# Four rounded weight buffers, the low part written over the raw tile, bias rows in three pieces

## What is computed

```python
def first_block(...):
    for i in range(DEPTH):
        j = i // N_MIXERS
        if i % N_MIXERS == 0:
            mix = retention(x, ret_w_in[j], ret_w_out[j])
        else:
            mix = dilated_attention(x, attn_w_in[j], attn_w_out[j], rel_bias)
        x = _layer_norm(DEEPNORM_ALPHA * x + mix, ln_gain[i, 0], ln_bias[i, 0])
        x = _layer_norm(DEEPNORM_ALPHA * x + swiglu_ffn(x, ffn_w_up[i], ffn_w_down[i]),
                        ln_gain[i, 1], ln_bias[i, 1])
    return x

def second_block(...):
    for l in range(DEPTH):
        h = rms_norm(x, norm1_g[l])
        proj = h @ w_in[l]
        ...
        mixed = jnp.concatenate([y_att, y_conv.astype(x.dtype), y_rnn.astype(x.dtype)], axis=-1)
        x = x + mixed @ w_out[l]
        h2 = rms_norm(x, norm2_g[l])
        x = x + peer(h2, peer_wq[l], peer_k1[l], peer_k2[l], peer_u[l], peer_v[l])
    return rms_norm(x, final_g)
```

## Time and profile before

| | |
|---|---|
| median of 3 runs | 2896.3 us (2894.7 to 2897.42) |
| profiled execution | 2887.31 us, span of the profile 2885.5 us |
| granted TensorE clock, mean | 0.994 |
| TensorE, VectorE, ScalarE busy | 2796.1, 1916.6, 1558.9 us |
| DMA | 480.26 MB, 166 GB/s over the span |

### The profile page before, as it was taken

One profiled execution on the slowest core, in us unless ns is written; L12 is line 12 of the kernel. 1 busy time (PEld: TensorE's weight loads), 2 busy tenths in 40 slices (PEclk: granted clock), 3 DMA queues, 4 the chain that ended last, 5 costly groups with the idle time before them and its releaser, 6 DMA issues.

```text
span 2885.5 us, 51650 instructions
## 1 busy us (share of the span) xinstructions
PE 2796.1 (97%) x18787; PEld 2539.2 (88%) x18787; DVE 1916.6 (66%) x3175; ACT 1558.9 (54%) x2817; POOL 22.7 (1%) x37
## 2 busy tenths in 40 slices
PE   8999999999999989999999999998999999999998
PEld 7988988898998879999998888887999999988886
DVE  5655554555555868987886555578699678855555
ACT  4455454555545564447775444456544677644444
POOL 0000000000000000000000000000000000000000
PEclk9999999999999999999999999999999999999999
DMA  6445557664555444554444555543455444455554
GB/s 231 147 146 180 187 167 194 173 165 143 168 184 165 131 136 164 179 175 139 140 139 163 192 191 189 190 164 110 160 172 179 156 143 141 140 196 190 191 192 146
DMA packets 158723, 480.26 MB, mean 166 GB/s; under 512 B 14608, under 2 KB 51472, under 8 KB 158192
## 3 DMA queue, kind: packets, MB, share of 16 engines
q1 hardware_dynamic: 154080, 460.38, 48.3%
q0 software_dynamic: 4352, 17.53, 2.8%
q10 hardware_dynamic: 144, 0.34, 0.0%
HBM read 477.02 MB, written 1.18 MB: 166 GB/s over the span
## 4 chain that ended last, share of the span: by engine, by line
PE 89%; DVE 6%; ACT 3%; issue 1%; DMA 0%; ACTq 0%; POOL 0%; DVEq 0%; POOLq 0%
PE ps L1570 27%; PE ps L1572 27%; PE ps L1571 26%; PE ps L2087 4%; DVE wl L872 2%; ACT wh L404 2%; DVE arena L1261 1%; PE ps L1689 1%; DVE xr L891 1%; PE ps L2053 0%; PE ps L1827 0%; PE ps L1870 0%; ACT arena L465 0%; DVE arena L1142 0%; DMA xr<-x_dram 0%
## 5 line engine op out<-in xcount | busy, mean ns | idle before, releaser
L872 DVE TENSOR_TENSOR wl<-raw,wh 128x1024 fp32r<-128x1024 f32 x878 | 1075.5, 1225 | 865.4 <-ACT wh L404 858.4
L404 ACT ACTIVATE wh<-raw 128x1024 fp32r<-128x1024 f32 x878 | 930.0, 1059 | 1235.0 <-PE ps L1572 1229.3
L1570 PE MATMUL ps<-xh,wh 128*128 128x256 f32 x3920 | 1135.5, 290 | 6.5 <-DVE wl L872 4.3
L1571 PE MATMUL ps<-xl,wh 128*128 128x256 f32 x3920 | 1110.2, 283 | 0.0
L1572 PE MATMUL ps<-xh,wl 128*128 128x256 f32 x3920 | 1109.6, 283 | 0.0
L1570 PEld LDWEIGHTS ps<-xh,wh 128*128 128x128 f32 x3920 | 752.2, 192 | 23.0 <-issue 10.7
L1571 PEld LDWEIGHTS ps<-xl,wh 128*128 128x128 f32 x3920 | 753.3, 192 | 0.3
L1572 PEld LDWEIGHTS ps<-xh,wl 128*128 128x128 f32 x3920 | 752.2, 192 | 0.0
L1570 PE MATMUL ps<-wh,mh 128*128 128x512 f32 x1304 | 513.5, 394 | 3.7 <-DVE ml L884 2.0
L1572 PE MATMUL ps<-wh,ml 128*128 128x512 f32 x1304 | 510.1, 391 | 0.0
L1571 PE MATMUL ps<-wl,mh 128*128 128x512 f32 x1304 | 509.0, 390 | 0.0
(11 more groups left out here) (287 smaller groups left out, 2023.0 us busy)
## 6 DMA issues: line engine op xcount, KB each, us to landing
raw<-stream_dram SPq DMA_DIRECT2D x878, 512.0 KB, 3.3
arena<-bias_scratch POOLq DMA_DIRECT2D x16, 384.0 KB, 7.9
arena<-norm_rows POOLq DMA_DIRECT2D x4, 1024.0 KB, 7.7
arena<-keys_dram POOLq DMA_DIRECT2D x2, 1024.0 KB, 5.0
arena<-ret_c_dram POOLq DMA_DIRECT2D x1, 1344.0 KB, 7.9
xr<-x_dram POOLq DMA_DIRECT2D x1, 1024.0 KB, 8.1
out_dram<-arena POOLq DMA_DIRECT2D x2, 512.0 KB, 2.9
arena<-rg_w_dram POOLq DMA_DIRECT2D x2, 256.0 KB, 2.9
```

The costliest lines, as they stand in the source:

```text
L404: A(wh[b % 2][:, :, :], raw[:, b % 4, :].rearrange("p (a b) -> p a b", a=DB), ACT.Copy) \
L872: V.tensor_tensor(wl[b % 2][:, :, :], raw[:, b % 4, :].rearrange("p (a b) -> p a b", a=DB), wh[b % 2][:, :, :].bitcast(F32), ALU.subtract) ...
L1570: M(out_ap, lh, rh, start=first, stop=False, skip_group_check=skip)
L1571: M(out_ap, lh, rl, start=False, stop=False, skip_group_check=skip)
```

## The change

The three things that it does: `wh` and `wl` get four buffers each. The four of `wl` lie in the same memory as the four slots of `raw`, so the subtraction writes over the raw tile that it reads. A slot is therefore free for the next load only when the matmuls of its tile are done, and SyncE waits for `mm_done` in place of `w_lo`; `hi(b)` waits for `mm_done` of tile b-4. The bias of a head comes in three transfers of 128 KB, one for each group, each behind the split of a tile of its own (`w_lo`), on GpSimd's queue as before. The order of all other instructions stays.

```diff
-        raw = sb("raw", [4, TILE])
-        wh = [sb(f"wh{i}", [DB, P], F32R) for i in range(2)]
-        wl = [sb(f"wl{i}", [DB, P], F32R) for i in range(2)]
+        with nc.sbuf_tensor("raw", [P, 4, TILE], F32) as raw:
+            pass
+        low = sb("wl", [4, DB, P], F32R)
+        wl = [low[:, i, :, :] for i in range(4)]
+        wh = [sb(f"wh{i}", [DB, P], F32R) for i in range(4)]
...
                 for b, g in enumerate(sources, first):
-                    sp.wait_ge(w_lo, b - 3)
+                    sp.wait_ge(mm_done, b - 3)
                     load(b % 4, g)
...
                     for s in range(4):
-                        sp.wait_ge(w_lo, i * 4 + (s - 3))
+                        sp.wait_ge(mm_done, i * 4 + (s - 3))
                         load(s, i * 4 + s)
...
             for h in range(AH):
-                if h >= 4:
-                    pool.wait_ge(a_b, h - 3)
-                else:
-                    pool.wait_ge(w_lo, START["att"] + 12 + 4 * h)
-                pool.dma_start(bs[:, h % 4, :, :], bass.AP(
-                    scratch.tensor, h * 384, [[1, P], [AH * 384, G3], [1, T]])).then_inc(b_in[h % 4], 16)
+                for g in range(G3):
+                    if h >= 4:
+                        pool.wait_ge(a_b, h - 3)
+                        pool.wait_ge(w_lo, START["att"] + 29 + 6 * ((h - 2) // 2) + 3 * (h % 2) + g)
+                    else:
+                        pool.wait_ge(w_lo, START["att"] + 12 + 4 * (3 * h + g) // 3)
+                    pool.dma_start(bs[:, h % 4, g, :], bass.AP(
+                        scratch.tensor, (g * AH + h) * 384, [[1, P], [1, T]])).then_inc(b_in[h % 4], 16)
...
-                if b >= 2:
-                    act.wait_ge(mm_done, (b - 1) + n * body)
-                A(wh[b % 2][:, :, :], raw[:, b % 4, :].rearrange("p (a b) -> p a b", a=DB), ACT.Copy) \
+                if b >= 4:
+                    act.wait_ge(mm_done, (b - 3) + n * body)
+                A(wh[b % 4][:, :, :], raw[:, b % 4, :].rearrange("p (a b) -> p a b", a=DB), ACT.Copy) \
                     .then_inc(w_hi, 1)
...
-                V.tensor_tensor(wl[b % 2][:, :, :], raw[:, b % 4, :].rearrange("p (a b) -> p a b", a=DB),
-                                wh[b % 2][:, :, :].bitcast(F32), ALU.subtract).then_inc(w_lo, 1)
+                V.tensor_tensor(wl[b % 4][:, :, :], raw[:, b % 4, :].rearrange("p (a b) -> p a b", a=DB),
+                                wh[b % 4][:, :, :].bitcast(F32), ALU.subtract).then_inc(w_lo, 1)
...
-                dve.wait_ge(b_in[h % 4], 16 * (h // 4 + 1))
+                dve.wait_ge(b_in[h % 4], 16 * G3 * (h // 4 + 1))
```

More of the change, by code:

```diff
@@ L1587, in tile_a @@
                         pe.wait_ge(n_lo, split_before[norm] + c + 1)
-                    ins = passes(ps_t[:, e % 2, 0:T], (wh[b % 2][:, c, :], wl[b % 2][:, c, :]),
+                    ins = passes(ps_t[:, e % 2, 0:T], (wh[b % 4][:, c, :], wl[b % 4][:, c, :]),
                                  (xh[:, c, :], xl[:, c, :]), c == 0, c == DB - 1)
@@ L1600, in tile_b @@
                         ins = passes(ps_a[:, 2 * c + h, :], (mh[:, s, t], ml[:, s, t]),
-                                     (wh[b % 2][:, 4 * h:4 * h + 4, :].rearrange("p a b -> p (a b)"),
-                                      wl[b % 2][:, 4 * h:4 * h + 4, :].rearrange("p a b -> p (a b)")),
+                                     (wh[b % 4][:, 4 * h:4 * h + 4, :].rearrange("p a b -> p (a b)"),
+                                      wl[b % 4][:, 4 * h:4 * h + 4, :].rearrange("p a b -> p (a b)")),
                                      first, last, skip=True)
@@ L1611, in last_pair @@
                     t = slice(c * P, (c + 1) * P)
-                    s, w = 2 * (u % 2) + j, (b + j) % 2
+                    s, w = 2 * (u % 2) + j, (b + j) % 4
                     if (j, c, h) == (1, 0, 0):
@@ L1631, in out_part @@
                         ins = passes(ps_a[:, 2 * c + h, :], (high[:, t], low[:, t]),
-                                     (wh[b % 2][:, kb:DB:2, :], wl[b % 2][:, kb:DB:2, :]),
+                                     (wh[b % 4][:, kb:DB:2, :], wl[b % 4][:, kb:DB:2, :]),
                                      first and kb == 0, False, skip=True)
@@ L1641, in last_parts @@
                     high, low = mixed(2 * part + kb)
-                    t, w = slice(c * P, (c + 1) * P), (b + h) % 2
+                    t, w = slice(c * P, (c + 1) * P), (b + h) % 4
                     if (h, c, kb) == (1, 0, 0):
```

## The result

The changed kernel takes 2840.84 us in the median of four runs (2836.79 to 2845.78); the kernel before, beside it, 2895.77 (2894.70 to 2897.42). The ratio is 0.9812, 95% interval 0.9801 to 0.9824: 54.9 us faster. A second measurement gave 2839.43 against 2894.83, ratio 0.981 (0.9797 to 0.9824).

What follows compares the result with a forecast made beforehand. Matmuls were taken as the bound, TensorE being busy for 97% of the span. Terms of 39.4 us won and 4 lost, 35.4 net, took the profile from 2887.3 to 2852; 9.0 more gave a median of 2861, range 2847 to 2881.

Steps and rivals of the forecast that it cites:

- A: First attention: scaling starts some 2 us sooner, so transposes and scores stop waiting; 8.9 us won, ends 0 and 10.
- B: Mixed stage of each second-block layer: shorter waits of transposes, at start and end; 12.6 us won, ends 4 and 17.
- C: Picking experts: one tile of lead evens out VectorE's uneven lots; 7.6 us won over two layers, ends 0 and 9.
- D: First gates: one-hots start 2.6 us earlier, the matmuls' stall and some lowered clock go; 5.8 us won, ends 0 and 7.
- E: Tile starts: TensorE's waits for `wl` outside the mixed stages and the third tile; 1.5 us won, ends 0 and 2.
- F: Value tables and down projections: some late first weight loads go if `wl` is the reason; 3 us won, ends 0 and 7.
- G: Loads beside GpSimd's 1 MB transfers (gains at start and feed-forwards): less slack; 3 us lost, three places at 1 each.
- H: Bias pieces: a load beside one takes 5.0 us, under 5.8 allowed; 1 us lost, ends 0 and 4.
- Only the tiles themselves gain: Rival: softmax chains get work sooner, but something else in the in-order queues comes last; 2880 us, chance 0.18.
- Buffers change nothing: Rival: `evacuate`, not the semaphore, holds `hi` everywhere, so only noise remains; 2896 us, chance 0.06.
- Loads become the bound: Rival: load, rounding and subtraction close a loop over three tiles; 2993 us at landings of 6.7 us, chance 0.06.
- the turning point: Landing time of loads, 6.4 us held over all 878 tiles, at which slower loads would cancel the 39 us won.

## Why the prediction was wrong

By its own terms, with the same stages of the two profiled executions, and of the second pair (the kernel before again, the changed one again, on two chips). Won is positive:

| term | predicted | first pair | second pair |
|---|---|---|---|
| A, first attention | 8.9 | 9.7 | 9.8 |
| B, mixed stages | 12.6 | 11.9 | 16.2 |
| C, picking | 7.6 | 9.9 | 9.8 |
| D, first gates | 5.8 | 5.9 | 7.8 |
| E and F, tile starts, tables, projections | 4.5 | 13.4 | 15.9 |
| G and H, feed-forwards, keys, bias | -4 | -1.9 | -1.3 |
| norms, first load, landing of the output | 0 | -1.1 | -1.3 |
| sum of the spans | 35.4 | 47.8 | 56.9 |

**The mechanism was right.** The lead of the rounding is the whole gain (2898.44 us without it), one tile of it is enough (2840.77 with three buffers), and each named sign is there: transposes, scores and gates no longer wait, the mixed stage keeps one long wait a layer, the feed-forward tile stays at 2.88 us (852 matmuls in 120 us, 851 before), some roundings wait for a landing, and a tile near the start of each feed-forward waits. The subtraction takes as long in place (1224 ns). One sign of being wrong came too, once: beside the bias pieces a load took 6.1 us where 5.8 were allowed, in the attention's values, and TensorE waited 0.35 us there.

**The step that failed is term F.** The prediction put it as "the first weight load of a tile comes late in 58 places, 10.0 us, most of it under matmuls that still run", took 3 and closed the term at 7. The two tables of values alone gave 8.2 us (10.5 in the second pair), retention 3.6 (4.0), and the first tiles of the tables 1.6: with E 13.4, 8.9 more than predicted, by far the largest miss. Its question, the late `wl` or the loop, is answered: the late `wl` (with and without the lead 1457 and 1439 matmuls in 330 us). What it missed is where the cost lies. In the first table before the change there are 227.9 ns in the mean between the matmuls on both sides of a tile's boundary, hardly more than the usual 226.5. The next interval is 259 once in every four tiles, and many of those behind it are 229 to 236. Worked out from the trace, the table takes 4.9 us more than 226.5 ns a matmul: 0.2 at the boundaries, 0.7 at one wait inside the last pair of tiles, 4.1 spread inside the tiles. Before, the low part was ready 0.23 us ahead of its tile in the median, now 2.1. The waits view shows the late weight loads but not this cost, for TensorE doesn't idle. The reading that would have: the smallest interval found anywhere between two such matmuls, times their count, against the stage's time. It should also have been applied to retention (16 + 16 tiles) and to the change from stage to stage, which the term left out. The feed-forward's tiles had 0.36 us of lead before, and between start and end of the stage six tiles take 16.98 us in place of 17.00: there the tile did gain nothing, as predicted.

**The second step is the one from the profile to the median.** It read "the median of the runs shown, 2896.3, lies 9.0 above it" and carried the 9.0 over to the changed kernel, whose median lies 1.3 above its profile: 7.7 us. In the kernel before again the profile stands 0.5 above the median. The profile that the prediction rested on was a quick execution with few stretches at 1.2 GHz, at a mean clock of 0.994; the eight runs of the kernel before again go with their clock, 2888.7 and 2889.2 us at 0.994, 2897.6 at 0.991. The changed kernel, profiled, is at 0.995. So a removed wait was priced at its length, where it also ends the drop of the clock behind it; the prediction counted one, 1.4 us in D. In the second pair B is 4.3 and D 1.9 above the first, and most of that is this. Together 12.4 in the sum and 7.7 in the offset are the 20 us between 2861 and 2840.8; either alone would have left the time in the range (2848.6, or 2853.3).

**The other terms.** A, B and D held within 0.8 us in the first pair. For B that is luck in part: 6.3 us were predicted for each layer, and 4.2 and 7.8 came. E, which wanted 1.5 of TensorE's waits at tile starts, can't be told apart in the sum: its waits went or became G's, but the third tile's, which was to stay at 1.5, grew to 2.1. C was bounded too low: "what is left is its own work, about 23.15", measured 23.04, against 23.73 before in each of six rounds of a layer, and a little in the tiles around. G's mechanism is shown for the two waits in the feed-forwards, and its size was small: the waits are 1.66, 1.89, 0.91 and 0.95 us, 5.4 in four places and not 3 in three; those beside the keys and the last norm's gain were not named. H's piece was allowed 5.0 us and met 6.1. Against them stands a gain in the feed-forwards that the prediction excluded ("more buffers bring nothing there"): without the stalls they take 187.4 us in place of 188.85, 1.5 each, most of it near the start (0.55) and in the last tiles (0.7). The low end of the range doesn't follow from its words either: B, F and D at their upper ends and the losses halved give 2861 - 11.6 = 2849, not 2847.

**The rivals.** *Only the tiles themselves gain* is out: A, B and D came as summed. *Buffers change nothing* is out with it. *Loads become the bound* was not reached, but was nearer than a chance of 0.06 says. The whole bias rows, unspaced, are enough to lose 48 us, and a load one tile later 205. Its formula left the tile's own matmuls out of the loop, so the price beyond the turning point goes by a quarter of L and not by a third; and from a tile's end to the matmuls there are 2.7 us beside the landing, not 2.4 (the run with late loads), which puts the turning point near 6.0 in place of 6.4.

## What to carry to other kernels

A row of 100% busy doesn't say that an engine runs at its best: count its instructions in a window, and compare the interval with the shortest one that the same form has elsewhere. A wait on the path is worth its length and what the clock does after it, and a single profile is one draw of that; set two beside each other before a difference between profile and median is carried over. When a buffer is shared to pay for another, look at once at every long transfer beside the loads that have become later, and cut and space those.

## What the hardware showed that was not expected

- TensorE's matmuls of 512 columns come every 226.5 ns when the low part has been ready for 2.1 us, and every 229.0 when it is ready 0.23 us before the tile, at full clock and without an idle moment. By tile the loss is 135 ns under 0.15 us of lead, 54 to 60 at 0.20 to 0.225, and 2 from 0.3 us on. The Trainium skill (TensorE: Matmul & The Clock Gate, Step-by-step: what each phase is for) has the sequencer take up the next instruction while the last still runs. That a semaphore which comes at the last moment leaves it nothing to take up would fit these intervals; it was argued and not shown.
- The same program, at the same place, gets 2.4 GHz in one execution and 1.2 GHz for about 3.4 us in the next. These places lie behind waits of TensorE, and the kernels with fewer waits had fewer of them (seven and eleven stretches before, four, five and six with the lead). Where loads came late over and over, with the bias rows whole, the mean clock of 206 us fell to 0.92.
- A load of 512 KB that lands in 3.3 us beside no transfer of GpSimd's took 8.5 to 11.7 us beside two of 384 KB, and the same bytes in six transfers of 128 KB held loads to 9.2.
